# Mixer of a fused two-block transformer: grams ahead of the turn of the values, turns and cross products behind the first inverse product, banks opened by the start flag

## The reference, cut to what matters

```python
def step(S, inp):
    r_t, w_t, k_t, v_t, kk_t, a_t = inp
    sa = jnp.einsum('bhvk,bhk->bhv', S, -kk_t)
    S = (S * w_t[:, :, None, :] + sa[..., None] * (kk_t * a_t)[:, :, None, :]
         + v_t[..., None] * k_t[:, :, None, :])
    return S, jnp.einsum('bhvk,bhk->bhv', S, r_t)
...
bonus = jnp.sum(rh * kh * r_k.astype(jnp.float32), -1, keepdims=True) * vh
out = (o + bonus).reshape(bsz, t_len, B_WIDTH).astype(p.dtype)
return out * g
...
x = x + jnp.concatenate([y_a, y_b], axis=-1) @ ev_w_out[j]
x = x + conv_glu_ffn(rmsnorm(x, ff_norm[layer]), ff_w_up[layer], ff_conv_w[layer],
                     ff_conv_b[layer], ff_w_down[layer])
```

## Time and profile before

| | |
|---|---|
| median of 3 runs | 1293.79 us (1290.83 to 1295.17) |
| profiled execution, span | 1296.9 us |
| PE busy, weight loads busy | 96%, 90% of the span |
| DVE, ACT, POOL busy | 73%, 56%, 1% |
| mean granted TensorE clock | 0.995 of 2.4 GHz |
| chain that ended last | PE 90%, DVE 4%, ACT 3%, issue 2%, DMA 1% |

### The profile page before, as it was taken

One profiled execution on the slowest core, in us unless ns is written; L12 is line 12 of the kernel. 1 busy time (PEld: TensorE's weight loads), 2 busy tenths in 40 slices (PEclk: granted clock), 3 DMA queues, 4 the chain that ended last, 5 costly groups with the idle time before them and its releaser, 6 DMA issues.

```text
span 1296.9 us, 24000 instructions
## 1 busy us (share of the span) xinstructions
PE 1251.3 (96%) x10155; PEld 1163.7 (90%) x10155; DVE 943.0 (73%) x1257; ACT 722.1 (56%) x1056; POOL 15.2 (1%) x26
## 2 busy tenths in 40 slices
PE   6999999999999999999998998999999999999998
PEld 6988879999989888999998997899998898899997
DVE  5875248888867766999986666699995676666553
ACT  6833358655665665866656555745454644644342
POOL 0011000000000000000000000000000000000000
PEclk9999899999999999999999999999999999999999
DMA  9450236877458426688763435599976366575550
GB/s 318 155 195 3 67 125 208 277 249 246 163 195 308 148 88 217 223 281 296 259 226 105 174 131 182 208 306 345 349 277 232 122 221 195 196 260 194 183 176 33
DMA packets 163877, 263.81 MB, mean 203 GB/s; under 512 B 5869, under 2 KB 98233, under 8 KB 163770
## 3 DMA queue, kind: packets, MB, share of 16 engines
q1 hardware_dynamic: 160586, 259.54, 58.4%
q10 hardware_dynamic: 3184, 2.73, 0.7%
HBM read 261.17 MB, written 1.05 MB: 202 GB/s over the span
## 4 chain that ended last, share of the span: by engine, by line
PE 90%; DVE 4%; ACT 3%; issue 2%; DMA 1%; SPq 0%; DVEq 0%; ACTq 0%
PE ps L1093 23%; PE ps L1064 16%; PE ps L1066 16%; PE ps L1065 16%; PE ps L2314 2%; PE ps L832 2%; PE ps L833 2%; PE ps L834 2%; PE ps L1079 1%; PE ps L1081 1%; PE ps L1080 1%; PE ps L812 1%; ACT whi L602 1%; DVE wlo L608 1%; DMA ring<-in_ev_w_in_dram 1%
## 5 line engine op out<-in xcount | busy, mean ns | idle before, releaser
L608 DVE TENSOR_TENSOR wlo<-ring,whi 128x2048 fp32r<-128x2048 f32 x194 | 443.0, 2288 | 106.7 <-ACT whi L602 106.7
L1064 PE MATMUL ps<-ghi,whi 128*128 128x256 f32 x1600 | 448.6, 280 | 0.8 <-DVE wlo L608 0.8
L1065 PE MATMUL ps<-glo,whi 128*128 128x256 f32 x1600 | 446.8, 279 | 0.0
L1066 PE MATMUL ps<-ghi,wlo 128*128 128x256 f32 x1600 | 446.5, 279 | 0.0
L602 ACT ACTIVATE whi<-ring 128x2048 fp32r<-128x2048 f32 x194 | 370.6, 1914 | 92.7 <-PE ps L1093 56.9
L1064 PEld LDWEIGHTS ps<-ghi,whi 128*128 128x128 f32 x1600 | 300.4, 188 | 2.3 <-DVE wlo L608 1.0
L1065 PEld LDWEIGHTS ps<-glo,whi 128*128 128x128 f32 x1600 | 299.7, 187 | 1.2
L1066 PEld LDWEIGHTS ps<-ghi,wlo 128*128 128x128 f32 x1600 | 300.4, 188 | 0.0
L1093 PE MATMUL ps<-whi,yhi 128*128 128x512 f32 x480 | 159.0, 396 | 3.1 <-DVE ylo L1973 1.3
L1093 PE MATMUL ps<-wlo,yhi 128*128 128x512 f32 x480 | 156.4, 391 | 0.0
L1093 PE MATMUL ps<-whi,ylo 128*128 128x512 f32 x480 | 155.9, 390 | 0.0
(11 more groups left out here) (310 smaller groups left out, 1601.6 us busy)
## 6 DMA issues: line engine op xcount, KB each, us to landing
arena<-in_w_ada_dram SPq DMA_DIRECT2D x48, 1024.0 KB, 6.0
ring<-in_ff_w_up_dram SPq DMA_DIRECT2D x44, 1024.0 KB, 7.7
ring<-in_w_gate_up_dram SPq DMA_DIRECT2D x44, 1024.0 KB, 7.3
ring<-in_ff_w_down_dram SPq DMA_DIRECT2D x10, 2048.0 KB, 7.9
ring<-in_w_down_dram SPq DMA_DIRECT2D x10, 2048.0 KB, 8.7
ring<-in_od_w_qkv_dram SPq DMA_DIRECT2D x6, 2048.0 KB, 8.2
ring<-in_w_qkv_dram SPq DMA_DIRECT2D x6, 2048.0 KB, 8.0
ring<-in_w_in_dram SPq DMA_DIRECT2D x6, 2048.0 KB, 7.8
```

The costliest lines, as they stand in the source:

```text
L608: e.tensor_tensor(shaped(WLO[i % NB], k), v, shaped(WHI[i % NB], k).bitcast(F32), ALU.subtract).then_inc(S["w_lo"], 1)
L1064: e.matmul(o, wh, h[0][:, k, :], start=k == 0, stop=False)
L1065: e.matmul(o, wh, h[1][:, k, :], start=False, stop=False)
L1066: x = e.matmul(o, wl, h[0][:, k, :], start=False, stop=k == NK - 1)
```

## The change

Five edits, in the order of the program:

1. The grams L of both chunks are issued directly behind the tile `("v", 1)`, ahead of the wait for the mixed values and of their turn. They take banks that are free by then (6, 7, and those of `("ya", 1)` and `("u", 1)`). The turned values take the banks of the value tiles themselves.
2. The turns of the keys (`turned_in`) and the cross products L12 (`cross`) move behind the first and the second product of the first inverse round: Y(1, 0), both turns, L12 of chunk 0, Y(1, 1), L12 of chunk 1, then `rest(0)`. L12 has its own semaphore, and ACT copies the turned keys before L12.
3. POOL clears LTc in place of DVE, ahead of its wait for the second bonus sum. DVE copies the grams first and multiplies the values by the bonus sums behind them.
4. `clear` is gone. The first matmul into each part of a bank carries start, the others don't. The products of X for chunk 1 that don't need S0 lose their place ahead of the partial sum and join the others behind it (`x_of`); the products of O for chunk 1 that don't need SA move behind the next partial sum (`o_of`).
5. The bank plan follows the new order.

```diff
                 ("g", 0), ("g", 1), ("r", 0), ("r", 1), "ws", ("u", 0), ("ya", 0), ("ya", 1), ("u", 1), ("v", 0),
-                ("rk", 0), ("rk", 1), ("v", 1), ("vt", 0), ("vt", 1)]:
+                ("rk", 0), ("rk", 1), ("v", 1)]:
         P.use(key, r())
-    r = Ring(range(8))
+    at = {key: P.at[key][0] for key in [("ya", 1), ("u", 1), ("v", 0), ("v", 1), ("rk", 0), ("rk", 1)]}
+    late = 6, 7, at["ya", 1], at["u", 1]
+    for (n, g), b in zip(TWO, late):
+        P.use(("L", n, g), b)
     for n in range(2):
-        for g in range(2):
-            P.use(("L", n, g), r())
-        for g in range(2):
-            P.use(("L12", n, g), r())
-    P.use(("tok", 0), r())
-    P.use(("tok", 1), r())
+        P.use(("vt", n), at["v", n])
+    r = Ring([6, 7, at["v", 0], at["v", 1], *late[2:], at["rk", 0], at["rk", 1]])
+    for key in [("Y", 1, 0), ("tok", 0), ("tok", 1), ("L12", 0, 0), ("L12", 0, 1), ("Y", 1, 1), ("L12", 1, 0), ("L12", 1, 1)]:
+        P.use(key, r())
     for i in range(1, 6):
-        for n in range(2):
-            P.use(("Y", i, n), r())
+        if i > 1:
+            for n in range(2):
+                P.use(("Y", i, n), r())
         for g in range(2):
...
                 eye(flat64(TTc[n]), S["tt_eye"])
+            e.wait_ge(S["tilted"], 6)
+            for n in range(2):
+                e.memset(flat64(LTc[n]), 0.0).then_inc(S["l_zero"], 1)
             e.wait_ge(S["rk_mm"], 2)
...
                     key = ("L12", n, g)
-                    e.wait_ge(S["gram"], n + 1)
+                    e.wait_ge(S["cross"], n + 1)
                     e.activation(L12[n][0:64, g], c3(ps_of(key)[0:64, 0:256], 4), ACT.Copy).then_inc(bank_sem(key), 1)
 
-            l12(0)
-            l12(1)
             for i, dst in enumerate((BTok, KTok)):
...
                 e.activation(dst, ps_of(("tok", i))[:, :], ACT.Copy).then_inc(bank_sem(("tok", i)), 1)
+            l12(0)
+            l12(1)
 
...
             mixed(6)
-            for q in range(2):
-                key, v = ("rk", q), Vm[:, 2 * q:2 * q + 2, :]
-                e.wait_ge(S["rk_mm"], q + 1)
-                e.wait_ge(S["v_turned"], 2)
-                e.tensor_tensor(v, v, c3(ps_of(key)[:, :], 2), ALU.mult).then_inc(bank_sem(key), 1)
 
...
                     e.wait_ge(S["tilted"], 6)
-                    if n == g == 0:
-                        e.memset(LTc[0][:, :], 0.0).then_inc(S["l_zero"], 1)
-                        e.memset(LTc[1][:, :], 0.0).then_inc(S["l_zero"], 1)
-                        e.wait_ge(S["l_zero"], 2)
+                    e.wait_ge(S["l_zero"], n + 1)
                     e.copy_predicated(LTc[n][:, g], mask64(C_S64, 4), lt)
...
                     e.copy_predicated(TTc[n][:, g], mask64(C_P64, 4), lt).then_inc(bank_sem(key), 1)
+            for q in range(2):
+                key, v = ("rk", q), Vm[:, 2 * q:2 * q + 2, :]
+                e.wait_ge(S["rk_mm"], q + 1)
+                e.wait_ge(S["v_turned"], 2)
+                e.tensor_tensor(v, v, c3(ps_of(key)[:, :], 2), ALU.mult).then_inc(bank_sem(key), 1)
             zeros = {("AK", 0): 1, ("AK", 1): 2, ("RB", 0): 3, ("RB", 1): 4, ("RK", 0): 5, ("RK", 1): 6}
...
             pe_tile(e, w, ("v", 1), 0, False)
+            half = [slice(0, 64), slice(64, 128)]
+            e.wait_ge(S["tilted"], 3)
+            for n in range(2):
+                ps = [opened(e, ("L", n, g)) for g in range(2)]
+                for j in range(4):
+                    for x, y, c in ((At, Bt, 0), (Bt, At, 256)):
+                        for b in range(2):
+                            for g in range(2):
+                                z = e.matmul(ps[g][half[b], c + 64 * j:c + 64 * j + 64], x[half[g], j, n, half[b]],
+                                             y[half[g], j, n, half[b]], start=True, stop=True)
+                z.then_inc(S["gram"], 1)
             e.wait_ge(*read_out(("v", 0)))
...
 
-            half = [slice(0, 64), slice(64, 128)]
-            e.wait_ge(S["tilted"], 3)
-            for n in range(2):
-                ps = [opened(e, ("L", n, g)) for g in range(2)]
+            def turned_in(i, src):
+                ps = opened(e, ("tok", i))
+                e.wait_ge(S["tilted"], 6)
                 for j in range(4):
-                    for x, y, c in ((At, Bt, 0), (Bt, At, 256)):
-                        for b in range(2):
-                            for g in range(2):
-                                e.matmul(ps[g][half[b], c + 64 * j:c + 64 * j + 64], x[half[g], j, n, half[b]],
-                                         y[half[g], j, n, half[b]], start=True, stop=True)
+                    x = e.transpose(ps[:, 128 * j:128 * j + 128], src[:, j, 0, :], ident)
+                x.then_inc(S["tok_turned"], 1)
+            def cross(n):
                 ps = [opened(e, ("L12", n, g)) for g in range(2)]
...
                                      At[half[g], j, n, half[1]], start=True, stop=True)
-                x.then_inc(S["gram"], 1)
-            e.wait_ge(S["tilted"], 6)
-            for i, src in enumerate((Bt, Kt)):
-                ps = opened(e, ("tok", i))
-                for j in range(4):
-                    x = e.transpose(ps[:, 128 * j:128 * j + 128], src[:, j, 0, :], ident)
-                x.then_inc(S["tok_turned"], 1)
+                x.then_inc(S["cross"], 1)
 
...
                     blocks(("Y", i, n), LTc[n], Tc[n], S["y_mm"])
+                    if i == 1:
+                        if n == 0:
+                            turned_in(0, Bt)
+                            turned_in(1, Kt)
+                        cross(n)
                 rest(i - 1)
...
 
-            def clear(ps, cols):
-                e.matmul(ps[:, 0:cols], CT[0:1, C_Y64:C_Y64 + 128], CT[0:1, 0:cols], start=True, stop=False)
-            def x_old(n):
+            def x_of(n):
                 for g in range(2):
...
                 e.wait_ge(*read_out(("vt", n)))
+                if n:
+                    e.wait_ge(*read_out("S0"))
                 ps = [opened(e, ("X", n, g)) for g in range(2)]
-                if n:
-                    for g in range(2):
-                        clear(ps[g], 256)
                 for j in range(4):
...
                             x = e.matmul(ps[g][half[b], 64 * j:64 * j + 64], AKm[n][:, g, j, half[b]],
-                                         VT[:, n, c:c + 64], start=n == 0, stop=n == 0)
-                return x
+                                         VT[:, n, c:c + 64], start=n == 0 or j == 0, stop=n == 0)
+                for j in range(4 * n):
+                    for g in range(2):
+                        for b in range(2):
+                            x = e.matmul(ps[g][half[b], 64 * j:64 * j + 64], At[half[g], j, 1, half[b]],
+                                         S0[half[g], j, :], start=False, stop=j == 3)
+                x.then_inc(S["x_mm"], 1)
 
...
                 x.then_inc(S["tt64_mm"], 1)
-            x_old(0).then_inc(S["x_mm"], 1)
+            x_of(0)
 
...
 
-            def o_old(n):
+            def o_of(n):
                 for g in range(2):
                     e.wait_ge(*read_out(("RK", n, g)))
-                clear(opened(e, ("O", n)), 512)
+                opened(e, ("O", n))
                 for h in range(8):
-                    o_part(n, h, VT[:, n, :], RKm, False, False)
+                    o_part(n, h, VT[:, n, :], RKm, h < 2, False)
                 if n:
...
                                      start=False, stop=False)
-            def o_new(n):
                 for g in range(2):
...
             x.then_inc(S["s0_mm"], 1)
-            x_old(1)
             sum_part(1, 0, first).then_inc(S["w_used"], 1)
-            e.wait_ge(*read_out("S0"))
-            for j in range(4):
-                for g in range(2):
-                    for b in range(2):
-                        x = e.matmul(ps_of(("X", 1, g))[half[b], 64 * j:64 * j + 64], At[half[g], j, 1, half[b]],
-                                     S0[half[g], j, :], start=False, stop=j == 3)
-            x.then_inc(S["x_mm"], 1)
-            o_old(0)
-            o_new(0)
+            x_of(1)
+            o_of(0)
             sa(1)
             second = taken(e, w)
-            o_old(1)
             sum_part(0, 2, second)
-            o_new(1)
+            o_of(1)
             variance(0)
```

## The result

| | before | after |
|---|---|---|
| median, runs taken together | 1293.6 us (6) | 1285.18 us (6), 1282.84 to 1288.54 |
| ratio, 95% interval | 1 | 0.9935 [0.9918, 0.9953] |
| profiled execution: span, mean clock | 1296.9 us, 0.995 | 1281.0 us, 1.000 |

A forecast was written before the change was run, and what follows sets the result against it. PE, busy 90% of the span, was taken as the bound. Gains of 5.5 us before the first T and 3.2 from the clears sum to 8.7, taking the median from 1293.8 to 1285.1 us, range 1281.5 to 1289.5.

The forecast's parts named there:

- The stretch up to the first T: From the last value tile's end to the first T: 10.6 us in place of 16.13, a gain of 5.5.
- 0.3 us for changes of shape: Before the first T: 0.3 us added to 10.3 for changes of tile shape, which show as short issue gaps.
- The waits: PE before the first T: DVE holds nothing up, slack 0.6 us at chunk 0's Y, 1.4 at the second L12.
- Zeros on POOL: Clearing LTc costs POOL 0.9 us, done by 85.5, over 10 us before DVE asks.
- The rounds: Five rounds of the inverse: same products and order, PE stays the bound at 6.83 us a round, cost and gain 0.
- The rival that entered them at 1.2 GHz: Five rounds: 64x64 products enter and stay at half clock, costing up to 34 us, 1319 in all; chance 0.04.
- the key turns lower it: First inverse round: turned keys and L12 let the clock fall to 1.2 GHz, costing 1.3 to 2.5 us; chance 0.12.
- The clears: S0's products to the last variance product: three clears on PE's chain removed, 3.16 us gained, taken as 3.2.
- The rival that they were hidden: Around X and SA of chunk 1: ACT's split and copies decide, PE arriving sooner waits; 1288.3 us, chance 0.11.
- The join: Half-clock stretch at 148 to 154 may fall on more or less work, bounded at some 1.5 us either way.
- That span is 3.1 us above the median: Last step: profiled span 1296.9 to 1288.2 us, so the median goes from 1293.8 to 1285.1.
- The 8.7 us forecast: Whole kernel: 5.5 us from the first stretch plus 3.2 from the clears.

The follow-up runs named there:

- Grams behind the turn: The changed kernel with the grams back behind the turn of the values, all else kept: 1289.11 us (9 runs), ratio 0.9954.
- bonus first: The changed kernel with DVE's bonus multiply back ahead of the masked copies, PE's order kept: 1291.92 us (10 runs), ratio 0.9981.
- turns first: The changed kernel with the key turns and both cross products back ahead of the first inverse product: 1287.0 us (9 runs), ratio 0.9944.
- before without clears: The kernel before with its three clears replaced by the start flag, products in their old positions, run twice: 1293.85 us (12), then 1291.76 us (12).
- with clears: The changed kernel with the three clears put back, new product order kept, run twice: 1290.84 us (11 runs), then 1287.08 us (6).
- zeros on DVE: The changed kernel with the two memsets of LTc back on DVE, directly ahead of the masked copies: 1287.36 us, one run.
- the three with ACT's new order: The changed kernel with two ACT places exchanged, alone or with chunk 0's first partial sum cut around SA, halves in either order: 1284.69, 1283.59, 1282.03 us.
- ACT's order: The changed kernel with ACT's copies of Y64 ahead of the weight split and those of TT64 ahead of X's copy: 1284.69 us (4 runs), ratio 0.9928.

## Why the prediction was right, step by step

**The stretch up to the first T** was forecast at 10.6 us and took 9.60, so 6.5 us less than before where I had 5.5. The terms: grams 2.32, took 2.42 with a gap of 0.08; turn 2.2, took 1.98; Y 1.08, took 1.08; both turns of keys 1.32, took 1.02; L12, Y, L12 2.28, took 2.01; `rest(0)` 1.09, took 1.09. The key turns and L12 were off for one cause: I took the duration of a record, which runs on past the start of the next (0.66 us for four turns), where the step to the next is what counts (1.02 us for eight, so 0.51 for four). The 0.3 us for changes of shape did not appear: no run shows this term, and the one gap in the stretch stands among the grams, where the kernel has no wait. It is 0.08 us here and 0.08 to 0.47 in the other profiles with the grams in this place; the prediction has it at nothing, and no run shows its cause. The waits came out as worked: slack of 0.62 for Y (0.6), no wait at the second L12, where the multiply ended at 95.99 + 1.27 = 97.26 and L12 was wanted at 98.36, 1.1 later (1.4). Grams behind the turn, the bonus first, and the turns first each gave back a wait of the size that those slacks say: 1.88 + 1.33, 3.50 and 0.88 us.

**What the first part is worth** is not the 6.5 us of the pair of profiles. The turn of before ran at 1.2 GHz in the profiled execution (3.45 us) and at 2.4 in another, in the second run of before without clears, whose first part is that of before:

```profile
92.76 2.02 PE L2279 MATMUL ps<-consts_sb,mix 128*128 128x128 f32 x16 [1.88 <-issue]
```

So 1.4 us of the 6.5 depend on the execution. That leaves 5.1; V end to T in that other profile is 14.72 us (90.88 to 105.60), 5.1 more than 9.60 and 4.8 more than 9.88, and the runs at a clock of 1.000 give 5.1 us too (with the new places of X and O in it, which are worth 0.2 us in the traces: 19.31 against 19.48 and 19.51). The forecast had 5.5. Two errors nearly cancel in it, and that was luck: 1.0 us too much for the new stretch (10.6 for 9.60), and for the old one 1.3 us of a slow turn (3.45 for 2.18) that not every run pays.

**Zeros on POOL** were hidden as forecast; POOL ended them at 81.83, over 10 us before DVE asks at 92.02:

```profile
80.84 0.99 POOL L1272 MEMSET pre<- 128x512 f32 x2 [32.90 <-DVE mix L1849]
```

**The rounds**: 31.22 us in both, at a clock of 1.00. The rival that entered them at 1.2 GHz did not happen in the profiles. Nor did the key turns lower it: over 90 to 100 us, with both kinds of turns in it, it is 1.00. The rule of the Trainium skill, TensorE: Matmul & The Clock Gate, section Part 4: PE-mode transpose, would have let the eight key turns count for less than products; here they are 1.02 us amid other products, and the clock did not fall. The trace doesn't contradict the rule for a longer run of them, which no version here has.

**The clears**: 3.16 forecast, 3.19 in the pair of profiles, 2.7 to 2.9 at a clock of 1.000 and 1.8 to 3.1 over all classes of clock. The rival that they were hidden falls with the chain of before without them (19.48 us for 22.50) and with their return in the changed kernel (22.45 for 19.31). It has a grain of truth: without the products' new places, 0.24 us of wait came in their stead.

**The join** took 2.37 us less in the pair of profiles, by the clock alone. The prediction bounded this at 1.5 us either way, which was too little: a full stretch at 1.2 GHz was there in one profile and absent in the other.

**The weak step** is the last, "That span is 3.1 us above the median". The span excludes some 1.8 us that the device time includes, so the profiled execution lay 4.9 us above its kernel's median, at a lower clock than most. The sum should have been made against an execution at the median's clock. The 1.8 us sit in both kernels and drop out of the difference; the part that comes from the clock does not, because the terms read at 1.2 GHz (turn, join) belong to some executions only. The 8.7 us forecast stand against 8.4 in the first comparison, 9.6 in the pool and 7.9 at a clock of 1.000; that they lie so near to 8.4 is partly the luck told above and the share of runs at each clock, which the prediction did not treat.

**Left open**: why more runs of the changed kernel stay at a clock of 1.000 (8 of 12 against 12 of 62). The idle time taken away may be the cause. The other versions that keep the first stretch short or nearly so have 7 of 17 (with clears), 3 of 9 (turns first), 0 of 1 (zeros on DVE) and 6 of 14 (the three with ACT's new order). Those with its waits have 3 of 24 (before without clears), 1 of 9 (grams behind the turn) and 0 of 10 (bonus first). With the changed kernel and before that is 24 of 53 against 16 of 105, so the two go together; that the idle time is the cause is not shown. In the profile of bonus first the clock fell not at that wait but around 72 us, ahead of it, and at the join. A version of the changed kernel with idle time alone was not run.

## What to carry to other kernels

Read at every wait on PE's chain which engine's queue is in the wrong order, and move a product whose inputs are ready into it: here taking back one reordering on DVE alone cost 3.5 us, and one on PE 2.9. A matmul that only zeroes a bank is not cheap: with one row of contraction 512 columns took 1.05 us, and the variance product with 128 rows and 512 columns took the same 1.05. The start flag on the first product of each part does it at no cost that the traces show. When an effect is below 0.5%, compare runs of equal mean clock and not medians alone, and when a filler waits although its inputs are there, look at which bank it opens.

## What the runs showed of the hardware that I had not expected

- The spread of this kernel goes with the mean clock: medians of 1291.47, 1293.33, 1296.02 and 1298.46 us at 1.000, 0.997, 0.996 and 0.993. The profiles show falls to 1.2 GHz at the same three places, each in some executions only: around 72 to 77 us (before, before without clears the first time, bonus first, ACT's order), at the turn behind 1.88 us of idle (before, before without clears the first time), and in the join (before, before without clears the second time, bonus first, zeros on DVE).
- Idle time ahead does not decide it. PE stood still for 1.88 us in before and the turn took 3.45 us; the same 1.88 us in "grams behind the turn" and in the second run of before without clears were followed by a turn of 2.02, and 3.50 us of waiting in "bonus first" by a clock of 1.00.
- Sixteen passes take 1.98 us in the turn of the values, eight take 1.02 in those of the keys: at full clock a pass of 128 columns steps in 0.12 to 0.13 us.
- Between 15 and 21 us the clock column shows 1.00 while the same product steps by 0.21 us at first and by 0.12 us later. The change comes at 18.2 us in one execution and at 21.4 in another, so that over 18 to 21 us PE gets through 26 or 16 matmuls.
